# The experts' gates as three bf16 one-hot products per token, with the one-hots of four tokens side by side

## The chip, the cores and the metric

One core of a Trainium2 chip runs the whole program. The metric is the device time of one execution in microseconds (us). The core has five engines that run side by side and meet at semaphores: TensorE (PE for its matmuls, PEld for its weight loads), VectorE (DVE), ScalarE (ACT), GpSimd (POOL) and SyncE (SP, which here only issues transfers).

## What is computed

A transformer block with a hybrid mixer, memory attention and an MLP, and then a second block with a state-space mixer and a product-key expert layer (PEER), for 256 tokens of width 1024. The change touches only the expert layer. Each token picks, in each of 8 heads, 16 experts out of 128 x 128; an expert's number is a pair (i1, i2) of key numbers, and each pick has a softmax weight:

```python
i1 = jnp.take_along_axis(i_half[:, :, 0], pos // PEER_TOPK, axis=-1)
i2 = jnp.take_along_axis(i_half[:, :, 1], pos % PEER_TOPK, axis=-1)
experts = (i1 * PEER_KEYS + i2).reshape(T, PEER_HEADS * PEER_TOPK)
gates = jax.nn.softmax(best, axis=-1).reshape(T, PEER_HEADS * PEER_TOPK)
...
u = expert_u[eb].astype(xb.dtype)
act = jax.nn.gelu(jnp.einsum('td,tkd->tk', xb, u), approximate=False) * gb
return jnp.einsum('tk,tkd->td', act, expert_v[eb].astype(xb.dtype))
```

The kernel gathers nothing. It computes the hidden value of all 16,384 experts for all tokens and multiplies each by a gate, which is 0 for an expert that the token didn't pick. So it needs, for each token, a 128 x 128 matrix of gates: the sum over the token's 128 picks of weight x onehot(i1) x onehot(i2).

## The kernel before

**The weight stream.** All large weights pass through four slots in blocks of 128 x 1024 float32. SP loads a block into `raw`; ACT casts it to its high part `wh` (L516); DVE subtracts to get the low part `wl` (L1106, the "split"); PE multiplies. One block of expert up-weights is used by `up`: 24 matmuls with 256 columns moving, three for each of 8 slices (high x high, high x low, low x high), into one of two banks of `AO`. ACT takes the result through Gelu into `hid` (L948), and then casts the block that is four ahead. All matmuls go through one helper line, L2090.

**The stage of the gates.** 128 blocks of up-weights make the expert layer. The first 64 have a stage of their own. The first 29 (`PLAIN`) run while DVE does the top-k. Then come 32 rounds: in round c PE does `up` of block 29 + c and then the gates of 8 tokens (`BATCH`), one matmul per token: the one-hot rows of i2 and the weighted one-hot rows of i1, with the picks on the partitions, both float32. ACT copies the 1024 columns of the result out of the double buffer `Y` into `gstage` (L970) and sends them to DRAM (`gate_spill`), from where windows of gates come back later. DVE writes the one-hots of round c + 1 and then splits block 29 + 4 + c. The one-hots have two buffers (`hots`): round c + 1's are written once round c - 1's product is done (`g_prod`), and PE waits for them with `hot` and `hot2`. After the 32 rounds three more `up` follow, and then 128 rounds in which up and down products alternate.

**How the one-hots are written before.** `picks` holds, for every pick (partition) and token, i1, i2 and the weight in float32; ACT copies it out of PSUM after a transpose (L960). `numbers` holds 0 to 127 on each partition. For 8 tokens DVE does one TENSOR_TENSOR over 1024 elements (is i2 equal to the number, L1809) and eight TENSOR_SCALAR over 128 elements (is i1 equal, times the weight, L1814).

The order of the work is written out by hand on every engine; nothing is planned by a program.

Of the kernel before, what the change touches and what calls it, by code (L numbers as in the profile page):

```python
# [23 lines left out]
P = 128  # L24
# [3 lines left out]
BF16 = mybir.dt.bfloat16  # L28
ACT = mybir.ActivationFunctionType
ALU = mybir.AluOpType  # L30
# [4 lines left out]
T = 256  # L35
TT = T // P
# [19 lines left out]
PEER_H, TOPK, KEYS = 8, 16, 128  # L56
# [2 lines left out]
AHEAD = 64  # L59
PLAIN = 29  # L60
BATCH = 8
BATCHES = T // BATCH
WIN = 16
WINDOWS = KEYS // WIN
# [79 lines left out]
def build(nc, stream, gain_cols, cols, rows, post_gains, x, mem, meta, keys_in, out, h2_spill):  # L144
    ctx = ExitStack()
    with ctx:
        def sb(name, shape, dt=F32):
            return ctx.enter_context(nc.sbuf_tensor(name, shape, dt))
# [18 lines left out]
        masks_at = (nc.sbuf_base + 31) // 32 * 32  # L167
# [5 lines left out]
        gain = sb("gain", [P, GAINS * KT])  # L173
        stat = sb("stat", [P, 48])
        choice_at = (nc.sbuf_base + 31) // 32 * 32
        picks = sb("picks", [P, 3, T])
        numbers = sb("numbers", [P, KEYS])
        arena_at = (nc.sbuf_base + 31) // 32 * 32
        arena = sb("arena", [P, 32 * BLK])
        row_pick = sb("row_pick", [P, 32])  # L180
# [2 lines left out]
        def at(name, shape, offset, dt=F32, base=None):  # L183
            return nc.alloc_sbuf_tensor_at(name, shape, dt, offset=(arena_at if base is None else base) + offset)
# [62 lines left out]
        QP = at("QP", [P, 16, T], 8768)  # L247
        hid = at("hid", [P, AHEAD, T], 0)
        gates = at("gates", [P, 2, BATCHES, WIN * BATCH], 65536)
        hots = at("hots", [P, 2, 2, BATCH, KEYS], 98304)  # L250
        gstage = at("gstage", [P, 2, KEYS, BATCH], 114688)
        up_l = at("up_l", [P, 2, T], 98304)
        up_s = at("up_s", [P, 2, T], 100352)
# [14 lines left out]
        gsum = at("gsum", [P, 2, TT * PEER_H], 114688)  # L268
        ranks = at("ranks", [P, TOPK + 1, HK], 114816, BF16)

        peer_ah = at("peer_ah", [P, 2, T], 0, F32R, base=x_at)
        peer_al = at("peer_al", [P, 2, T], 2048, F32R, base=x_at)

# [6 lines left out]
        Y = ps("Y", [P, TT, D])  # L280
        AO = ps("AO", [P, 2, 512])
        M = ps("M", [P, 2, 512])
# [59 lines left out]
        top_sub, top_exp, top_nat, top_turn, top_T = (sem(n) for n in (  # L342
            "top_sub", "top_exp", "top_nat", "top_turn", "top_T"))
        indexed, hot, g_prod, g_out = sem("indexed"), sem("hot"), sem("g_prod"), sem("g_out")
        hot2, curve, up_part = sem("hot2"), sem("curve"), sem("up_part")
# [31 lines left out]
        TAIL = P0 + AHEAD + 2 * PAIRED  # L377
        gate_spill = nc.dram_tensor("gate_spill", (P, BATCHES, KEYS * BATCH), F32).ap()

# [125 lines left out]
        def _(act):  # L505
            step = Steps(act, act_step)
# [105 lines left out]
            for j in range(8):  # L612
                k = AG_ORDER[j]
# [342 lines left out]
            for c in range(EXP_AT, PLAIN):  # L956
                if c == FIRST_TURN:
                    act.wait_ge(top_turn, 1)
                    for j in range(TT):
                        nc.scalar.copy(picks[:, :, P * j:P * j + P],  # L960
                                       M[:, j, 0:3 * P].rearrange("p (n t) -> p n t", n=3)).then_inc(top_T, 1)
                hidden(c, P0 + c, c)
                split(P0 + 4, c)

            def gates_out(c, s):

                act.wait_ge(g_prod, c + 1)
                if not (type(c) is int and c < 2):
                    act.wait_ge(g_stored[s], (c - s) * 8)
                nc.scalar.copy(gstage[:, s, :, :],  # L970
                               Y[:, s, :].rearrange("p (t k) -> p k t", t=BATCH)).then_inc(g_out, 1)
                act.wait_ge(g_out, c + 1)
                act.dma_start(gate_spill[:, c, :], gstage[:, s, :, :].rearrange("p k t -> p (k t)"))\
                    .then_inc(g_stored[s], 16)

            def gates_in(w, first=0, n=BATCHES):

# [21 lines left out]

            for c in range(BATCHES):  # L1000
                with_gates(c, c)
                for p in range(len(PARTS)):
                    if c == PARTS[p][1] + 1:
                        part_in(p)
            for c in range(PLAIN + BATCHES, AHEAD):
                hidden(c, P0 + c, c)
# [51 lines left out]
            for w in range((KEYS - PAIRED) // WIN):  # L1058
# [10 lines left out]
                if ends[1]:  # L1069
                    for s in range(4):  # L1070
                        c = 4 * (g1 - 1) + s
# [26 lines left out]
        def _(dve):  # L1098
            step = Steps(dve, vec_step)
# [124 lines left out]
            for j in range(8):  # L1224
                split(STREAM["ag"] + 4, j)
                if j % 2:
                    c = j // 2
# [389 lines left out]
            for k in range(16):  # L1617
                c, s = divmod(k, 8)
# [114 lines left out]
            for j in range(TT):  # L1733
                for a0, a1, w, o in ROWS:
                    n = a1 - a0
# [34 lines left out]
            for j in range(TT):  # L1770
# [11 lines left out]
                for n in (8, 4, 2, 1):  # L1782
                    step.wait()
                    for half in range(2):
                        a, b = eqs[:, half, 0:n, :], eqs[:, half, n:2 * n, :]
# [18 lines left out]
            def one_hots(c):  # L1804

                s = c % 2
                if c >= 2:
                    dve.wait_ge(g_prod, c - 1)
                nc.vector.tensor_tensor(hots[:, s, 0, :, :], numbers[:, None, :].to_broadcast([P, BATCH, KEYS]),  # L1809
                                        picks[:, 1, c * BATCH:c * BATCH + BATCH][:, :, None]  # L1810
                                        .to_broadcast([P, BATCH, KEYS]), ALU.is_equal).then_inc(hot2, 1)
                for t in range(BATCH):
                    k = c * BATCH + t
                    ins = nc.vector.tensor_scalar(hots[:, s, 1, t, :], numbers[:, :], picks[:, 0, k:k + 1],  # L1814
                                                  picks[:, 2, k:k + 1], ALU.is_equal, ALU.mult)
                ins.then_inc(hot, 1)

            one_hots(0)
            for c in range(FIRST_TURN, PLAIN):
# [5 lines left out]
            for c in range(PLAIN + BATCHES, AHEAD - 1):  # L1825
                split(P0 + 4, c)
                if c < PLAIN + BATCHES + 2:
                    b = c - PLAIN - 2
# [71 lines left out]
            for w in range((KEYS - PAIRED) // WIN):  # L1900
# [10 lines left out]
                if ends[1]:  # L1911
                    for s in range(4):
                        c = 4 * (g1 - 1) + s
# [18 lines left out]
        def _(pool):  # L1932
            step = Steps(pool, pool_step)
# [131 lines left out]
            for p in range(3):  # L2065
# [10 lines left out]
            norm(5)  # L2076
            pool.wait_ge(spilled, 16)
            pool.wait_ge(tile_scaled, 3 * len(NORMS))
            nc.gpsimd.iota(numbers[:, :], [[1, KEYS]], base=0, channel_multiplier=0,
                           allow_small_or_imprecise_dtypes=True).then_inc(indexed, 1)  # L2080
            nc.gpsimd.iota(ranks[:, :, :], [[1, TOPK + 1], [0, HK]], base=0, channel_multiplier=0,
                           allow_small_or_imprecise_dtypes=True).then_inc(indexed, 1)
# [5 lines left out]
        def _(pe):  # L2088
            def mm(o, a, b, start, stop):
                return nc.tensor.matmul(o, a, b, start=start, stop=stop)  # L2090
# [352 lines left out]
            for c in range(2):  # L2443
                ins = mm(M[:, 1, P * (c + 1):P * (c + 2)], RA[:, c, :], upper[:, :], True, True)
# [102 lines left out]
            for k in range(16):  # L2547
                c, s = divmod(k, 8)
# [7 lines left out]
                for t in range(3):  # L2556
                    h = 3 * s + t
                    ins = mm(yd[:, SSD_D * h:SSD_D * h + SSD_D], MM[:, k % 2, t, :],
                             XDT[:, c, SSD_D * h:SSD_D * h + SSD_D], True, True)
# [27 lines left out]
            for j in range(14):  # L2587
                kt = (j - SC_T) % 16
                b = STREAM["wout2"] + j
                pe.wait_ge(split_lo, b + 1)  # L2590
                for c in range(TT):
                    if j < SC_T:
                        pe.wait_ge(sc_lo, j + 1)
                    else:
                        pe.wait_ge(y_lo, 3 * c + kt // 4 + 1)
                    ins = flat(b % SLOTS, [Y4[c]], [m2h[:, kt, P * c:P * c + P]], [m2l[:, kt, P * c:P * c + P]],
                               (0, 512), j == 0, False)
# [44 lines left out]
            for j in range(TT):  # L2642
                for n in range(3):
                    ins = nc.tensor.transpose(M[:, j, P * n:P * n + P], NAT[:, j, n, :], ident[:, :])
# [5 lines left out]
            def with_gates(c, s, i=0):  # L2650

                pe.wait_ge(a_free, i * 4 + (A_BASE["peer"] + PLAIN + s - 1))
                up(s, P0 + PLAIN + s, (PLAIN + s) % 2, 0, i)
                if not (type(c) is int and c < 2):
                    pe.wait_ge(g_out, c - 1)
                pe.wait_ge(hot2, c + 1)
                pe.wait_ge(hot, c + 1)
                for t in range(BATCH):
                    ins = mm(Y[:, s % 2, KEYS * t:KEYS * t + KEYS], hots[:, s % 2, 0, t, :], hots[:, s % 2, 1, t, :],
                             True, True)  # L2660
                ins.then_inc(g_prod, 1)

            for s in range(4):
# [33 lines left out]
            for j, halves in ((0, (0, 1)), (1, (0,)), (1, (1,))):  # L2697
                for s in range(2):
                    b = N_BLOCKS - 2 + s
                    pe.wait_ge(split_lo, b + 1)  # L2700
                    pe.wait_ge(hid_lo, KEYS - 1 + s + FF_CHUNKS)
                    ins = flat(b % SLOTS, [[Y4[j][h] for h in halves]], [peer_ah[:, s, P * j:P * j + P]],
                               [peer_al[:, s, P * j:P * j + P]], [512 * h for h in halves], False, s == 1)
# [75 lines left out]
```

## Time and profile before

| what | value |
|---|---|
| median of 3 runs | 1435.97 us (1435.6 to 1437.34) |
| the profiled execution's own time | 1436.53 us |
| its span in the trace | 1434.8 us |
| mean granted TensorE clock | 0.997 of full speed |
| busy in the span: PE, DVE, ACT | 1407.3, 1075.0, 794.5 us |
| the 32 rounds with gates | about 747 to 893 us from the span's start |

The profile comes from one execution; its times are counted from the start of its span. "Busy" is the time in which at least one instruction of the engine ran. Consecutive instructions of an engine overlap a little in the records, so what one costs in a row of many is read from the distance of starts, not from its own duration. A float32 matmul shows as two records, each with a weight load of its own.

### The profile page before, as it was taken

The numbers are of one execution on the slowest core, as the hardware profiler recorded it, in microseconds if no ns is written. First come the engines' busy times: TensorE is split into PE (matmuls) and PEld (weight loads), VectorE is DVE, ScalarE is ACT, GpSimd is POOL, SyncE is SP. The second block draws the span as 40 slices with busy tenths as digits, with TensorE's granted clock in tenths as the row PEclk, the third lists the DMA queues.
The fourth block names the chain that finished last, engine by engine and source line by source line (L and its number), as shares of the span: only waits on it lengthen the run. The fifth ranks groups of instructions, "written<-read, shape, count | busy, mean of one in ns | idle before, by whom it ended". The sixth has DMA issues, their size and how long they took to land.

```text
span 1434.8 us, 25922 instructions
## 1 busy us (share of the span) xinstructions
PE 1407.3 (98%) x8623; PEld 1251.4 (87%) x8623; DVE 1075.0 (75%) x2058; ACT 794.5 (55%) x1303; POOL 68.7 (5%) x66
## 2 busy tenths in 40 slices
PE   8999999999999999999999999999999999999998
PEld 8988878888898888799999999888888888888886
DVE  6996776666687588599999997666666666677776
ACT  6766764545576535455554555555555555554454
POOL 0100000000003521000000000000000000000000
PEclk9999999999999999999999999999999999999999
DMA  7533335565444523654656787657557575577754
GB/s 294 189 119 127 113 132 190 190 192 188 132 148 150 174 89 118 191 176 155 203 188 221 259 261 250 213 191 248 192 188 251 188 252 187 196 246 253 256 190 146
DMA packets 103098, 274.38 MB, mean 191 GB/s; under 512 B 8320, under 2 KB 40816, under 8 KB 102528
## 3 DMA queue, kind: packets, MB, share of 16 engines
q1 hardware_dynamic: 65024, 237.16, 49.6%
q10 hardware_dynamic: 37664, 34.37, 7.3%
q0 software_dynamic: 352, 2.11, 0.5%
q8 instruction: 32, 0.52, 0.2%
q14 instruction: 26, 0.21, 0.0%
HBM read 254.67 MB, written 18.87 MB: 191 GB/s over the span
## 4 chain that ended last, share of the span: by engine, by line
PE 85%; DVE 8%; ACT 3%; issue 1%; SPq 1%; DMA 1%; POOL 0%; DVEq 0%; ACTq 0%
PE Y L2090 43%; PE AO L2090 39%; DVE wl L1106 2%; PE M L2090 2%; DVE CV L1213 1%; ACT wh L516 1%; SPq L488 1%; DVE XS L1493 1%; DVE X L1346 0%; DVE xn L1343 0%; DVE xhl L1138 0%; DMA X<-in_x 0%; ACT xhl L559 0%; DMA raw<-in_stream 0%; ACT junk L550 0%
## 5 line engine op out<-in xcount | busy, mean ns | idle before, releaser
L1106 DVE TENSOR_TENSOR wl<-raw,wh 128x1024 fp32r<-128x1024 f32 x440 | 543.3, 1239 | 197.8 <-ACT wh L516 197.3
L2090 PE MATMUL AO<-xhl,wh 128*128 128x256 f32 (+3 forms) x2784 | 648.8, 315 | 4.6 <-DVE xhl L1138 2.6
L516 ACT CAST wh<-raw 128x1024 fp32r<-128x1024 f32 x440 | 460.8, 1050 | 146.7 <-PE Y L2090 72.5
L2090 PEld LDWEIGHTS AO<-xhl,wh 128*128 128x128 f32 x2784 | 455.3, 188 | 37.0 <-issue 3.2
L2090 PE MATMUL AO<-xhl,wl 128*128 128x256 f32 (+2 forms) x1776 | 485.0, 282 | 0.0
L2090 PEld LDWEIGHTS AO<-xhl,wl 128*128 128x128 f32 x1776 | 333.9, 188 | 7.9
L2090 PE MATMUL Y<-wh,peer_al 128*128 128x512 f32 x512 | 199.2, 389 | 0.0
L2090 PE MATMUL Y<-wl,peer_ah 128*128 128x512 f32 x512 | 199.2, 389 | 0.0
L2090 PE MATMUL Y<-wh,peer_ah 128*128 128x512 f32 x512 | 199.2, 389 | 0.0
L990 ACT CAST peer_ah<-hid 128x256 fp32r (+1 forms) x128 | 52.0, 406 | 178.3 <-DVE hid L1837 93.5
L2090 PEld LDWEIGHTS Y<-wl,peer_ah 128*128 128x128 f32 x512 | 96.1, 188 | 20.1
L2090 PEld LDWEIGHTS Y<-wh,peer_al 128*128 128x128 f32 x512 | 96.1, 188 | 20.0
L2090 PEld LDWEIGHTS Y<-wh,peer_ah 128*128 128x128 f32 x512 | 96.2, 188 | 17.6
L1843 DVE TENSOR_TENSOR peer_al<-hid,peer_ah 128x256 fp32r<-128x256 f32 x128 | 54.4, 425 | 71.7 <-ACT peer_ah L990 71.5
L948 ACT ACTIVATE hid<-AO 128x256 f32<-128x256 f32 (+1 forms) x64 | 24.6, 384 | 90.9 <-PE AO L2090 90.8
L1814 DVE TENSOR_SCALAR hots<-numbers,picks 128x128 f32<-128x128 f32 x256 | 68.3, 340 | 0.0
L2090 PE MATMUL Y<-hots 128*128 128x128 f32 x512 | 62.3, 275 | 0.0
L2090 PEld LDWEIGHTS Y<-hots 128*128 128x128 f32 x512 | 60.0, 192 | 0.0
L1962 POOL TENSOR_SCALAR stat<-stat 128x1 f32<-128x1 f32 x12 | 6.6, 548 | 1087.5 <-ACT fin_j L1084 814.6
L1837 DVE TENSOR_TENSOR hid<-hid,gates (+1 forms) x128 | 53.4, 417 | 1.6 <-issue 0.7
L2090 PE MATMUL Y<-wh,mlp_ah 128*128 128x512 f32 x128 | 50.1, 391 | 1.2 <-DVE mlp_al L1415 1.2
L1213 DVE SCALAR_TENSOR_TENSOR CV<-UP,colp,CV 128x256 f32<-128x256 f32 x120 | 49.8, 475 | 0.3 <-ACT CV L604 0.3
(354 smaller groups left out, 1610.4 us busy)
## 6 DMA issues: line engine op xcount, KB each, us to landing
raw<-in_stream SPq DMA_DIRECT2D x440, 512.0 KB, 3.3
gate_spill<-gstage ACTq DMA_DIRECT2D x32, 512.0 KB, 4.9
gates<-gate_spill ACTq DMA_DIRECT2D x6, 2048.0 KB, 15.2
gates<-gate_spill ACTq DMA_DIRECT2D x6, 512.0 KB, 7.1
rowg<-in_post SPq DMA_DIRECT2D x3, 512.0 KB, 4.3
X<-in_x SPq DMA_DIRECT2D x2, 512.0 KB, 5.0
memx<-in_mem SPq DMA_DIRECT2D x1, 1024.0 KB, 7.6
keys<-in_keys POOLq DMA_DIRECT2D x1, 1024.0 KB, 7.0
```

What stands on the lines that cost most here:

```text
L488: sp.dma_start(RV[o:o + 1, :, :].bitcast(F32), RS[f:f + HG, c, :].bitcast(F32)).then_inc(lines_in, 16)
L516: nc.scalar.copy(wh[:, s, :], raw[:, s, :]).then_inc(split_hi, 1)
L948: nc.scalar.activation(hid[:, c, :], AO[:, s % 2, 0:T], ACT.Gelu).then_inc(a_free, 1)
L990: nc.scalar.copy(peer_ah[:, s, :], hid[:, slot, :]).then_inc(hid_hi, 1)
L1106: nc.vector.tensor_tensor(wl[:, s, :], raw[:, s, :], wh[:, s, :].bitcast(F32), ALU.subtract)\
L1213: nc.vector.scalar_tensor_tensor(out=CV[:, c, :], in0=src, scalar=col("conv_w", c * CONV_W + w), in1=CV[:, c, :], op0=ALU.mult, op1=ALU.ad ...
L1493: nc.vector.scalar_tensor_tensor(out=dst, in0=src, scalar=wt, in1=dst, op0=ALU.mult, op1=ALU.add).then_inc(xconv, 1)
L1814: ins = nc.vector.tensor_scalar(hots[:, s, 1, t, :], numbers[:, :], picks[:, 0, k:k + 1], picks[:, 2, k:k + 1], ALU.is_equal, ALU.mult)
L1837: nc.vector.tensor_tensor(h, h, gates[:, w % 2, :, bass.ds(k * BATCH, BATCH)], ALU.mult)\
L1843: nc.vector.tensor_tensor(peer_al[:, s, :], hid[:, slot, :], peer_ah[:, s, :].bitcast(F32), ALU.subtract).then_inc(hid_lo, 1)
L1962: nc.gpsimd.tensor_scalar(stat[:, dst:dst + 1], stat[:, src:src + 1], EPS, None, ALU.add).then_inc(done, 1)
L2090: return nc.tensor.matmul(o, a, b, start=start, stop=stop)
```

## The change

The gate matrix of a token becomes three bf16 matmuls that add up in PSUM. The stationary side of each is the plain one-hot of i2, the same for all three; the moving side is the one-hot of i1 times one of three bf16 parts of the weight (the weight rounded to bf16, the rest rounded again, and what is left), which together make the weight. DVE writes the plain one-hots of i1 and i2 for 8 tokens with one TENSOR_TENSOR of 2048 bf16 elements into `found`, waits for it, and writes the three weighted ones with three TENSOR_TENSOR of 1024 bf16 elements into `spread`. The elements of four tokens (`QUAD`) lie side by side, so that a token's row of 128 is read by PE with a step of four elements (8 bytes). ACT writes `picks` in bf16, and DVE makes the weight's second and third part once, in the first round. `numbers` becomes 128 x 4 bf16 elements, each number four times. All buffers that change lie in memory that was free at that time; the arena starts at the same address.

```diff
-        picks = sb("picks", [P, 3, T])
-        numbers = sb("numbers", [P, KEYS])
+        picks = sb("picks", [P, BATCHES, 2 * 5, QUAD], BF16)
+        rest = sb("rest", [P, TT, P])
...
-        hots = at("hots", [P, 2, 2, BATCH, KEYS], 98304)
+        spread = at("spread", [P, 2, 3, 2, KEYS, QUAD], 98304, BF16)
+        found = at("found", [P, 2, 4, KEYS, QUAD], 122880, BF16)
...
+        numbers = at("numbers", [P, KEYS, QUAD], 0, BF16, base=masks_at)
...
-                        nc.scalar.copy(picks[:, :, P * j:P * j + P],
-                                       M[:, j, 0:3 * P].rearrange("p (n t) -> p n t", n=3)).then_inc(top_T, 1)
+                        b = BATCHES // TT * j
+                        nc.scalar.copy(picks[:, b:b + BATCHES // TT, 0:6, :].rearrange("p b (n h) q -> p b n (h q)", n=3),
+                                       M[:, j, 0:3 * P].rearrange("p (n b t) -> p b n t", n=3, t=BATCH)).then_inc(top_T, 1)
...
-                nc.vector.tensor_tensor(hots[:, s, 0, :, :], numbers[:, None, :].to_broadcast([P, BATCH, KEYS]),
-                                        picks[:, 1, c * BATCH:c * BATCH + BATCH][:, :, None]
-                                        .to_broadcast([P, BATCH, KEYS]), ALU.is_equal).then_inc(hot2, 1)
-                for t in range(BATCH):
-                    k = c * BATCH + t
-                    ins = nc.vector.tensor_scalar(hots[:, s, 1, t, :], numbers[:, :], picks[:, 0, k:k + 1],
-                                                  picks[:, 2, k:k + 1], ALU.is_equal, ALU.mult)
+                nc.vector.tensor_tensor(found[:, s, :, :, :], numbers[:, None, :, :].to_broadcast([P, 4, KEYS, QUAD]),
+                                        picks[:, c, 0:4, None, :].to_broadcast([P, 4, KEYS, QUAD]), ALU.is_equal)\
+                    .then_inc(hot2, 1)
+                if c == 0:
+                    parts_of_weights()
+                dve.wait_ge(hot2, c + 1)
+                for n in range(3):
+                    ins = nc.vector.tensor_tensor(spread[:, s, n, :, :, :], found[:, s, 0:2, :, :],
+                                                  picks[:, c, 4 + 2 * n:6 + 2 * n, None, :]
+                                                  .to_broadcast([P, 2, KEYS, QUAD]), ALU.mult)
                 ins.then_inc(hot, 1)
+
+            def parts_of_weights():
+
+                w = [picks[:, :, 4 + 2 * n:6 + 2 * n, :].rearrange("p b h q -> p b (h q)") for n in range(3)]
+                r = rest[:, :, :].rearrange("p j (b t) -> p (j b) t", t=BATCH)
+                for j in range(TT):
+                    b = slice(BATCHES // TT * j, BATCHES // TT * (j + 1))
+                    step(nc.vector.tensor_tensor(r[:, b, :], M[:, j, 2 * P:3 * P].rearrange("p (b t) -> p b t", t=BATCH),
+                                                 w[0][:, b, :], ALU.subtract))
+                step.wait()
+                step(nc.vector.tensor_copy(w[1], r))
+                step.wait()
+                step(nc.vector.tensor_tensor(w[2], r, w[1], ALU.subtract))
+                step.wait()
...
-            nc.gpsimd.iota(numbers[:, :], [[1, KEYS]], base=0, channel_multiplier=0,
+            nc.gpsimd.iota(numbers[:, :, :], [[1, KEYS], [0, QUAD]], base=0, channel_multiplier=0,
...
                 for t in range(BATCH):
-                    ins = mm(Y[:, s % 2, KEYS * t:KEYS * t + KEYS], hots[:, s % 2, 0, t, :], hots[:, s % 2, 1, t, :],
-                             True, True)
+                    h, q = divmod(t, QUAD)
+                    for n in range(3):
+                        ins = mm(Y[:, s % 2, KEYS * t:KEYS * t + KEYS], found[:, s % 2, 2 + h, :, q],
+                                 spread[:, s % 2, n, h, :, q], n == 0, n == 2)
                 ins.then_inc(g_prod, 1)
```

On DVE, at the start of the rounds, stood before (the last row of the top-k, the last split ahead of it, and rounds 0 and 1):

```order
L1794 TENSOR_TENSOR NAT<-BV,gsum 128x128
L1106 TENSOR_TENSOR wl<-raw,wh 128x1024 [waits split_hi]
L1809 TENSOR_TENSOR hots<-numbers,picks 128x1024 [waits top_T]
L1814 TENSOR_SCALAR hots<-numbers,picks 128x128 x8
L1106 TENSOR_TENSOR wl<-raw,wh 128x1024 [waits split_hi]
```

and stands now, with the round that then repeats as the last four rows:

```order
L1813 TENSOR_TENSOR found<-numbers,picks 128x2048 [waits top_T]
L1831 TENSOR_TENSOR rest<-M,picks 128x128 x2
L1834 CAST picks<-rest 128x32x8 [waits vec_step]
L1836 TENSOR_TENSOR picks<-rest,picks 128x32x8 [waits vec_step]
L1820 TENSOR_TENSOR spread<-found,picks 128x1024 [waits hot2,vec_step]
L1820 TENSOR_TENSOR spread<-found,picks 128x1024 x2
L1106 TENSOR_TENSOR wl<-raw,wh 128x1024 [waits split_hi]
L1813 TENSOR_TENSOR found<-numbers,picks 128x2048 [waits g_prod]
L1820 TENSOR_TENSOR spread<-found,picks 128x1024 [waits hot2]
L1820 TENSOR_TENSOR spread<-found,picks 128x1024 x2
```

Nine instructions of a round become four, the second of which waits for the first, and four instructions with three waits stand once in the first round, ahead of the first product.

On PE, at the end of one round's `up` and the start of the next, stood before:

```order
L2090 MATMUL AO<-xhl,wh 128x256 x2
L2090 MATMUL AO<-xhl,wl 128x256
L2090 MATMUL Y<-hots 128x128 [waits hot,hot2]
L2090 MATMUL Y<-hots 128x128 x7
L2090 MATMUL AO<-xhl,wh 128x256 [waits split_lo,a_free]
```

and stands now:

```order
L2111 MATMUL AO<-xhl,wh 128x256 x2
L2111 MATMUL AO<-xhl,wl 128x256
L2111 MATMUL Y<-spread,found 128x128 [waits hot,hot2]
L2111 MATMUL Y<-spread,found 128x128 x23
L2111 MATMUL AO<-xhl,wh 128x256 [waits split_lo,a_free]
```

Eight float32 matmuls of a round become 24 bf16 matmuls at the same place, with the same waits.

## Rows read from the trace of the kernel before

**Rows 1.** The page: busy time, share of the span and instructions of each engine
```profile
PE 1407.3 (98%) x8623; PEld 1251.4 (87%) x8623; DVE 1075.0 (75%) x2058; ACT 794.5 (55%) x1303; POOL 68.7 (5%) x66
```

**Rows 2.** The chain that ended last, 735 to 920 us: start, us, what
```profile
741.82 5.68 PE AO L2090 x48
747.50 1.78 PE Y L2090 x16
749.29 2.84 PE AO L2090 x24
...
890.93 1.78 PE Y L2090 x16
```

**Rows 3.** Busy time of each engine in the stretch of the rounds
```profile
747.50:892.72 145.22, 145.22 (x1259) 145.22 (x1258) 136.48 (x311) 73.78 (x95) 0.00 (x0) 1.00 0.76 248
```

**Rows 4.** Instructions on the tile hots: ns min/median/max, first and last start us
```profile
L2090 PEld LDWEIGHTS Y<-hots x512: 189/192/192, 747.2 to 892.3; 128*128 128x128 f32 x171
L2090 PE MATMUL Y<-hots x512: 272/275/275, 747.3 to 892.4; 128*128 128x128 f32 x171
```

**Rows 5.** Timeline of DVE, an early and a late round: start, us, what
```profile
747.20 1.22 DVE L1809 TENSOR_TENSOR hots<-numbers,picks 128x1024 f32<-128x1024 f32 x1
748.33 2.14 DVE L1814 TENSOR_SCALAR hots<-numbers,picks 128x128 f32<-128x128 f32 x8
750.38 1.22 DVE L1106 TENSOR_TENSOR wl<-raw,wh 128x1024 fp32r<-128x1024 f32 x1
751.52 1.22 DVE L1809 TENSOR_TENSOR hots<-numbers,picks 128x1024 f32<-128x1024 f32 x1
...
883.06 1.23 DVE L1106 TENSOR_TENSOR wl<-raw,wh 128x1024 fp32r<-128x1024 f32 x1 [0.21 <-ACT wh L516]
```

**Rows 6.** Timeline of DVE in the top-k, instructions on bf16 tiles
```profile
709.11 2.36 DVE L1773 TENSOR_TENSOR eqs<-PF,ranks 128x2048 bf16<-128x2048 bf16 x2
...
712.97 1.22 DVE L1779 TENSOR_TENSOR eqs<-eqs,I16B 128x2048 bf16<-128x2048 bf16 x1
...
717.51 1.28 DVE L1787 TENSOR_TENSOR eqs<-eqs 128x1024 bf16<-128x1024 bf16 x2
...
724.57 0.29 DVE L1787 TENSOR_TENSOR eqs<-eqs 128x256 bf16<-128x256 bf16 x1
724.89 0.49 DVE L1787 TENSOR_TENSOR NAT<-eqs 128x128 f32<-128x128 bf16 x2
```

**Rows 7.** TensorE where less than 128 columns move per load, and its cheapest full load
```profile
507.20 0.78 PE L2090 MATMUL Y<-XDT,MM 128*128 128x64 f32 x6
507.81 0.86 PE L2090 MATMUL M<-ST,XS 128*128 128x384 f32 x2
421.56 0.54 PEld L2090 LDWEIGHTS M<-dtz,upper 128*128 128x128 f32 x4
L2180 PEld LDWEIGHTS M<-ident x128: 138/140/231, 2.6 to 375.7; 128*128 128x128 f32 x128
```

**Rows 8.** Around the first round, and DVE instructions like the new ones there
```profile
740.27 0.63 DVE L1794 TENSOR_TENSOR NAT<-BV,gsum 128x128 f32<-128x128 f32 x2
741.86 0.86 ACT L960 COPY picks<-M 128x384 f32<-128x384 f32 x2 [0.22 <-PE M L2644]
742.82 1.22 DVE L1809 TENSOR_TENSOR hots<-numbers,picks 128x1024 f32<-128x1024 f32 x1
...
898.09 0.29 DVE L1830 COPY gates<-gstage 128x256 f32<-128x256 f32 x1
...
901.25 0.43 DVE L1837 TENSOR_TENSOR hid<-hid,gates 128x256 f32<-128x256 f32 x1
```

**Rows 9.** The busiest window of transfers in the rounds, and the spill's landing
```profile
789.00:805.00 16.00, 16.00 (x141) 16.00 (x140) 15.12 (x37) 8.48 (x12) 0.00 (x0) 1.00 0.93 302
gate_spill<-gstage ACTq DMA_DIRECT2D x31, 512.0 KB, 4.9
```

More of the change, by code:

```diff
@@ L61 @@
 BATCH = 8
+QUAD = BATCH // 2
 BATCHES = T // BATCH
```

## The prediction

> **What bounds the kernel now.** The page's busy times come first: PE is busy for 1407 of 1434.8 us, DVE for 1075 [rows 1]. That is an average over many stages, so next the chain that ended last, at the place of the change. From 741.82 to 892.7 us it holds nothing but PE: 2.84 us of `up` (24 matmuls on AO), 1.78 us of gate products (16 records on Y), and so on, 32 times [rows 2]. The window of just this stretch agrees: PE busy for 145.22 of 145.22 us, DVE for 136.48, ACT for 73.78 [rows 3]. So a round takes 2.84 + 1.78 = 4.62 us, PE's work alone sets it, and whatever shortens the product shortens the round, until another engine's round is longer.
>
> The next engine is DVE, and the timeline says how close it is. Early in the stage it is never idle: it starts one-hots at 747.20 and the next at 751.52, so its own round takes 4.32 us (1.13 for L1809, 2.05 for the eight L1814, 1.14 for the split). Later it idles some 0.2 us per round for ACT's cast, because PE only frees a slot every 4.62 us [rows 5]. DVE is thus 0.30 us per round off being the bound. The reader should see that a faster product alone could give only those 0.30 us; what DVE's new round costs decides as much.
>
> **PE's part.** Removed: 8 float32 matmuls per round, 16 records in 1.78 us, 111.5 ns each [rows 2, 4]. Added: 24 bf16 matmuls that each load 128 columns and move 128. No row shows a bf16 matmul, so it is bounded.
> - What moves: a float32 matmul of 128 columns costs 223 ns here (two records), one of the fp32r matmuls of `up` moves 256 columns in 2.84 / 24 = 118.3 ns [rows 2]. Half of that is 59 ns for 128 columns; a quarter of 223 is 56.
> - What loads: where little moves, the load sets the pace. Six records with 64 float32 columns start at 507.20 and the next form at 507.81, 102 ns each, though 64 columns move in half of what 128 need, 56 ns. Four loads with only 24 columns moving take 0.54 us, and one takes 0.19, so 0.35 / 3 = 117 ns apart [rows 4, 7]. A float32 load therefore costs 102 to 117 ns, and if a bf16 load did too, the new product would be slower. But the load of the transposes, also 128 columns, is 140 ns long where the others are 189 to 192, some 50 ns less [rows 4, 7]: a full load can be had for about 52 to 67 ns, which hides nearly behind 59.
>
> I take 59 ns, because bf16 is half the bytes of float32 and so nearer to the short load; the bounds are 56 and 117. The product costs 24 x 59 = 1.42 us, PE's round 2.84 + 1.42 = 4.26 us, 0.36 less. It breaks even at 1.78 / 24 = 74 ns.
>
> On this the Trainium skill speaks with two voices. Its page "TensorE: Matmul & The Clock Gate", section "Back-to-back issue gap", gives some 81 ns per matmul of 128 columns in a stream in which every matmul has a load, and 56 ns without loads; by 81 the product would be 1.94 us and the kernel about 5 us slower. The same page, section "LDWEIGHTS (loading the stationary operand)", has a load take its columns / 1.2 ns, 107 ns here, which the float32 rows fit and the transposes' row doesn't; by that the kernel would be some 25 us slower. Its section "Weight-path perf modes — Fast Weight Load (FWL) and DoubleRow" promises a cheaper load for types other than FP32. No row here can choose between them.
>
> **DVE's part.** All lengths come from the top-k, which has bf16 instructions of just these sizes, one of them with one operand spread over a dimension [rows 6]. Two of 2048 elements take 2.36 us and one takes 1.22, so they start 1.14 apart and overlap by 0.08. Two of 1024 take 1.28, so they start 0.60 apart. An instruction that waits for the one before it starts 0.03 after its end (724.57 + 0.29 to 724.89). The new round: `found` 1.22 + 0.03, three `spread` 3 x 0.60, the split 1.14 as before, in all 4.19 us against 4.32. Not shown is an operand whose rows of 4 elements are read over and over. If that cost nothing, 4.19 stands; if all four lost the doubled bf16 rate, the round would be the float32 one, 2.27 + 3 x 1.14 + 1.14 = 6.83 us. I take 4.19, since L1779, with rows of 8 and an operand read over and over, keeps the rate.
>
> So PE's 4.26 stays just above DVE's 4.19. If DVE gets 0.1 longer than this, it is the bound.
>
> **The first round.** ACT's two copies have as many elements as before and let DVE start at 742.82 [rows 8]. Then `found` 1.25, two subtractions of 128 elements 0.63 + 0.03, a cast of 256 0.29 + 0.03, a subtraction of 256 0.43 + 0.03, three `spread` 0.60 + 0.60 + 0.68: ready at 747.39, where PE's product began at 747.50 by the chain, with its first load at 747.2 [rows 2, 4, 8]. PE may stand for 0 to 0.4 us, I take 0.2. Behind it DVE's split and second one-hots end at about 747.4 + 1.1 + 1.25 + 1.9 = 751.6, and PE's second product is due at 747.6 + 4.26 = 751.9, so the wait isn't repeated.
>
> **What costs nothing.** ACT does what it did: 73.78 us in 145 [rows 3]; shorter rounds leave it over 1.9 us free in each. The larger iota of `numbers` on GpSimd runs long before the top-k ends. Transfers: a round moves as many bytes in 4.26 us as in 4.62, so the mean share of 0.76 becomes 0.82 [rows 3]; a window of 16 us with 0.93 and 302 GB/s left PE fully busy [rows 9]. A spill lands in 4.9 us [rows 9], and its buffer is used again two rounds later, 8.5 us less the copy. With that cover gone, ACT's copy would wait, and its cast, DVE's split and PE's `up` behind it.
>
> **The sum.** 32 x (1.78 - 1.42) = 11.5 us less, or 11.8 unrounded (1.784, 1.416), and 0.2 more for the first round: -11.6. The profiled execution took 1436.53 us, so 1424.9, and it lies 0.56 above the median: 1424.4 us, by the median of the runs shown.
>
> **The rivals.**
> - **The load sets the pace of the products (slower).** A bf16 load costs what a float32 one does, 102 to 117 ns. The product takes 2.45 to 2.81 us, each round 0.67 to 1.03 more than before: +21 to +33 us, 1457 to 1469. For it: both float32 rows where little moves [rows 7]. Against it: the transposes' shorter load. Chance 0.10.
> - **The load, or the 8-byte step in which PE reads, is hidden in part.** 68 to 85 ns, around the middle between 59 and 102: the product takes 1.63 to 2.04 us, -5 to +8 us, 1431 to 1444. No row has PE read with a step. Chance 0.11: 0.04 of it faster, 0.02 no change, 0.05 slower.
> - **DVE becomes the bound.** The wait for `found` or the short rows cost 0.1 to 0.3 us more: rounds of 4.3 to 4.5 us, 1426 to 1432. Rows 5 speak for it: DVE has so little to spare. Chance 0.08. If the bf16 rate is lost, rounds of 6.83 us, +70 us, 1506: chance 0.04.
> - **The gain is hidden behind the transfers.** The rounds stay near 4.5 to 4.6 us since the spill and the weight stream come no faster: 1432 to 1436. The landing time of 4.9 us speaks against it. Chance 0.04, half of it no change.
>
> **How the numbers follow.** My forecast has the remaining 0.63; its own range is 1422 to 1429 (56 ns, where DVE's 4.19 is the floor and 0.43 x 31 = 13.3 us is the most to be had; 66 ns). Down to 1421 if DVE is a little cheaper, and up to 1437 with the longer DVE round, the transfers and the better half of the partly hidden load, it is 0.63 + 0.08 + 0.04 + 0.06, about 8 in 10. Changes of under 0.2% (2.9 us) are about what a measurement of this kernel can't tell from none. Faster by more: 0.63 + 0.08 + 0.02 + 0.04 = 0.77; within: 0.02 + 0.02 = 0.04; slower: 0.10 + 0.05 + 0.04 = 0.19.
>
> **What would show it.** In the profile after: 24 records on Y per round, 59 ns apart, and rounds 4.26 us long in the chain. If the chain's pieces on Y are longer than 1.78 us, the load rival holds, and PEld starts will be over 74 ns apart. If `found` is longer than 1.3 us or `spread` than 0.75, or the chain leaves PE for DVE's `spread`, it is DVE. If ACT waits before L970 for `g_stored`, it is the transfers. At the start, PE's idle time before the first product should be under 0.4 us. The most likely mistake is the price of a bf16 matmul with its load, which rests on no row of its own kind.

## The result, and the profile after

The changed kernel is slower: 1470.28 us, the median of 4 runs (1469.26 to 1471.28), against 1435.78 us of the kernel before (4 runs, 1434.68 to 1437.34). The ratio is 1.0239, with a 95% interval of 1.0222 to 1.0257. The prediction, 1424.4 us and so a gain, had the wrong sign, and the result lies 33 us above its range.

The page of the changed kernel, its busy times (those of before are in [rows 1]):

```profile
span 1467.4 us, 26279 instructions
PE 1441.0 (98%) x8879; PEld 1283.4 (87%) x8879; DVE 1074.4 (73%) x1902; ACT 794.7 (54%) x1303; POOL 69.6 (5%) x66
```

DVE and ACT are as busy as before to within 1 us; PE has 34 us more. The chain that ended last at the first rounds, beside [rows 2] (start us, us, what):

```profile
746.35 2.85 PE Y L2111 x24
749.20 2.84 PE AO L2111 x24
752.03 2.85 PE Y L2111 x24
```

It is PE alone, as before. `up` (AO) has kept its 2.84 us; a product (Y) takes 2.85 us where it took 1.78 and where 1.42 were forecast. Its 24 matmuls are 2.85 / 24 = 119 ns apart, twice the 59 ns of the prediction. (Times per matmul below are such pieces of the chain divided by the number of matmuls.) The window of the stretch, beside [rows 3] (stretch, us, busy us and instructions of PE, PEld, DVE, ACT and POOL, granted clock, DMA share, GB/s):

```profile
746.35:927.00 180.65, 180.65 (x1528) 177.85 (x1527) 136.27 (x157) 74.94 (x96) 0.00 (x0) 1.00 0.58 202
```

PE never idles, and the clock is at its full level of 2.4 GHz. The 32 rounds, from 746.35 to where `up` follows the last product at 925.36, take 179.0 us instead of 145.2: 33.8 more, and 32 x (2.85 - 1.78) gives 34. The span grew by 32.6, since this execution came to its first product 1.15 us earlier. So the whole loss is in the product, and nothing came back or was lost elsewhere.

Who uses the new tiles (duration ns min/median/max, first and last start us):

```profile
L2111 PEld LDWEIGHTS Y<-spread,found x768: 111/117/137, 746.2 to 924.9; 128*128 128x128 bf16 x192
L2111 PE MATMUL Y<-spread,found x768: 282/298/302, 746.2 to 925.1; 128*128 128x128 bf16 x192
L1820 DVE TENSOR_TENSOR spread<-found,picks x96: 683/686/695, 744.1 to 916.5; 128x1024 bf16<-128x1024 bf16 x96
L1813 DVE TENSOR_TENSOR found<-numbers,picks x32: 1218/1226/1228, 741.6 to 914.0; 128x2048 bf16<-128x2048 bf16 x32
```

A load record is now 117 ns long, and the matmuls of a product are 119 ns apart. From these rows alone the load looks guilty: this is just what the load rival forecast (102 to 117 ns apart, 1457 to 1469 us). But PEld starts once per matmul whichever of the two is late, so neither its spacing nor the 98% of the stretch in which it is "busy" says who waits for whom. PE reads both sides with the step of 8 bytes, and only experiments separate three causes: the load itself, the step of the loaded side, the step of the moving side.

### The profile page after: what moved, and what is told of

It is laid out like the page before. It is cut to its first block, busy times and chain, and to the rows that moved or that the text cites. A ratio compares the mean times of both kernels' runs of the same rounds, so it can differ in the third digit from the quotient of the medians.

```text
span 1467.4 us, 26279 instructions
## 1 busy us (share of the span) xinstructions
PE 1441.0 (98%) x8879; PEld 1283.4 (87%) x8879; DVE 1074.4 (73%) x1902; ACT 794.7 (54%) x1303; POOL 69.6 (5%) x66
## 4 chain that ended last, share of the span: by engine, by line
PE 86%; DVE 8%; ACT 3%; issue 1%; SPq 1%; DMA 1%; POOL 0%; DVEq 0%; ACTq 0%
PE Y L2111 44%; PE AO L2111 38%; DVE wl L1110 2%; PE M L2111 2%; DVE CV L1217 1%; ACT wh L519 1%; SPq L491 1%; DVE XS L1497 1%; DVE X L1350 0%; DVE xn L1347 0%; DMA X<-in_x 0%; DVE xhl L1142 0%; ACT xhl L562 0%; DMA raw<-in_stream 0%; ACT junk L553 0%
## 5 line engine op out<-in xcount | busy, mean ns | idle before, releaser
L2111 PE MATMUL Y<-spread,found 128*128 128x128 bf16 x768 | 96.1, 297 | 0.0
L2111 PEld LDWEIGHTS Y<-spread,found 128*128 128x128 bf16 x768 | 85.5, 117 | 2.8
L1820 DVE TENSOR_TENSOR spread<-found,picks 128x1024 bf16<-128x1024 bf16 x96 | 60.7, 688 | 1.1
L974 ACT COPY gstage<-Y 128x1024 f32<-128x1024 f32 x32 | 32.5, 1015 | 47.9 <-PE Y L2111 47.9
```

Of the source, the lines that this page charges most:

```text
L974: nc.scalar.copy(gstage[:, s, :, :], Y[:, s, :].rearrange("p (t k) -> p k t", t=BATCH)).then_inc(g_out, 1)
L1820: ins = nc.vector.tensor_tensor(spread[:, s, n, :, :, :], found[:, s, 0:2, :, :], picks[:, c, 4 + 2 * n:6 + 2 * n, None, :] .to_broadcast( ...
```

## The experiments

Three theories stood at the start: (A) the step of 8 bytes on the moving side (`spread`) slows the matmul; (B) the step on the stationary side (`found`) slows the load; (C) a bf16 load costs as much as a float32 one in any layout. Where no number of runs is given, there was one. Each group of runs has its own time of the kernel before beside it; across groups, small differences are read from the traces' rows and not from the times.

**One side at a time, then both.** A token's 128 elements are read from 128 neighbouring places of the same buffers, the step being kept on the other side.

```diff
 # moving side close together (and, for the stationary side, the same with found)
-                                 spread[:, s % 2, n, h, :, q], n == 0, n == 2)
+                                 spread[:, s % 2, n, h, :, :].rearrange("p k q -> p (k q)")[:, KEYS * q:KEYS * q + KEYS], n == 0, n == 2)
```

Expected with the moving side close together:

> PE takes the moving side of each bf16 product from 128 elements that lie close together in the same buffer; the stationary side keeps its step of four elements, and DVE writes as before. The output is not the reference's, since the elements read are not a token's. Theory A (reading the moving side with an 8-byte step halves its rate): the matmuls start 56 to 65 ns apart, a round is 4.2 to 4.4 us, the time near 1425 to 1430 us. Theory B (the stepped stationary load sets the pace) and theory C (any bf16 load of 128 columns costs about 118 ns): the pieces on Y stay 2.85 us, 1468 to 1472 us.

Expected with the stationary side close together:

> The stationary side alone is read from 128 elements close together; the moving side keeps the step of four. The output is not the reference's. Theory A (moving step): no change, 118 ns per matmul, 1468 to 1472 us. Theory B (stepped load): 56 to 65 ns per matmul, 1425 to 1430 us. Theory C (any bf16 load): no change.

Expected with both:

> Both sides are read from elements close together. The output is not the reference's. Theories A and B: 56 to 65 ns per matmul, 1425 to 1430 us, even where only one of the sides mattered or both must be close. Theory C (any bf16 load of 128 columns costs 118 ns): no change, 1468 to 1472 us.

Measured: 1424.43, 1468.5 and 1422.85 us, beside 1434.93 for the kernel before. The chain of the kernel with the moving side close together:

```profile
802.26 1.38 PE Y L2111 x24
803.63 2.89 PE AO L2111 x24
```

and its load records, whose stationary side is still stepped:

```profile
L2111 PEld LDWEIGHTS Y<-spread,found x768: 110/113/133, 746.6 to 880.2; 128*128 128x128 bf16 x192
```

The chain with only the stationary side close together, and its load records:

```profile
800.99 2.83 PE AO L2111 x24
803.83 2.79 PE Y L2111 x24
```
```profile
L2111 PEld LDWEIGHTS Y<-spread,found x768: 95/115/118, 747.5 to 924.2; 128*128 128x128 bf16 x192
```

and with both sides close together, its chain and its load records:

```profile
802.40 2.89 PE AO L2111 x24
805.29 1.36 PE Y L2111 x24
```
```profile
L2111 PEld LDWEIGHTS Y<-spread,found x768: 95/98/100, 745.7 to 878.6; 128*128 128x128 bf16 x192
```

One edit of the moving side brings the product from 2.85 to 1.38 us and the kernel from 1470 to 1424 us; the other edit takes 0.06 us off the product. The matmuls are where theory A put them, and B and C fall; the times, 1424.43 and 1422.85 us, are 1 to 2 us under the 1425 to 1430 expected. Load records of 113 ns stand beside matmuls that are 57 ns apart, so a record's length isn't what a load costs in a row of many, just as [rows 4] had 189 ns records 111.5 ns apart. Nor does the length tell of the load's own step: side by side the records are 98 ns long where the moving side is close together too, and 115 ns where it isn't. The step of the stationary side lengthens a record from 98 to 113 ns and costs 0.02 us of the product (1.38 against 1.36 us). What a bf16 load costs by itself no run shows: in such a row it is hidden at 57 ns.

The prediction had weighed two figures of the page "TensorE: Matmul & The Clock Gate" of the Trainium skill. Its section "Back-to-back issue gap" gives 81 ns for a matmul of 128 columns in a stream with loads and some 56 ns without them, and its section "LDWEIGHTS (loading the stationary operand)" gives 107 ns for the load. The trace agrees with neither 81 nor 107: here each of the 24 matmuls had a load of 128 columns, and they were 57 ns apart.

**Which step is dear?** Both sides at 4 bytes; the moving side at 6 bytes (96 places, so some tokens share columns); the moving side at 16 bytes (over both groups of four). Number and shape of the instructions stay.

```diff
 # moving side at 6 bytes; at 16 bytes the same with u=8 over both groups of four
+                                 spread[:, s % 2, n, h, 0:96, :].rearrange("p k q -> p (k q)").rearrange("p (k u) -> p k u", u=3)[:, :, min(q, 2)], n == 0, n == 2)
```

Expected at 4, 6 and 16 bytes:

> Both sides are read with a step of two elements (4 bytes) in place of four (8 bytes). The output is not the reference's. If the cost of a step grows with the bytes that it passes over, the matmuls are between 60 and 100 ns apart, 1426 to 1458 us; if any step breaks the pairs of bf16 elements, 118 ns as with four, 1468 to 1472 us; theory C: no change.

> The change with the moving side read with a step of three elements (6 bytes), the stationary side still four. The output is not the reference's. If the rate falls once a step passes over more than 4 bytes, 118 ns per matmul and 1468 to 1470 us; if it falls in proportion from 4 bytes on, about 88 ns and 1447 us; if it falls only at 8 bytes, 58 ns and 1424 us.

> The change with the moving side read with a step of eight elements (16 bytes), the stationary side still four. The output is not the reference's. If the half rate at four elements is a second level that holds for every longer step, 118 ns and 1468 to 1470 us; if the cost grows in proportion to the bytes, some 225 ns, products of 5.4 us per round and about 1555 us.

Measured: 1423.9, 1449.02 and 1615.7 us. One product in the chain of each, in this order:

```profile
805.62 1.39 PE Y L2111 x24
```
```profile
807.57 2.16 PE Y L2111 x24
809.73 2.86 PE AO L2111 x24
```
```profile
757.88 5.54 PE Y L2111 x24
763.42 4.22 PE AO L2111 x24
...
803.27 4.71 PE AO L2111 x24
807.98 5.54 PE Y L2111 x24
```

| step of the moving side, bytes | 2 | 4 | 6 | 8 | 16 |
|---|---|---|---|---|---|
| ns per matmul of 128 bf16 columns | 57 | 58 | 90 | 119 | 231 |
| the same / (128 columns x step), ns per column and byte | 0.22 | 0.113 | 0.117 | 0.116 | 0.113 |

(The column of 2 bytes is the run with the moving side close together, that of 8 bytes the change itself.) Up to 4 bytes the step is free; the run with 4 bytes missed its expectation, which had no price under 60 ns. From there the time of a column is 0.113 to 0.117 ns times the step in bytes, as if PE ran over the memory from the first to the last element, 16 bytes in 1.8 to 1.9 ns. A price per line of 16 bytes that is touched would give the same table; only a step of more than 16 bytes would tell the two apart, and no run has one. The page "SBUF — State Buffer" of the Trainium skill, section "Door 1: The DMA port swizzle (why `[64,N]` ≈ `[32,N]`)", has lines of 16 bytes that run at full rate from two hits per line on, with 8 bf16 elements as the free distance. For what TensorE moves, the table says otherwise: at 8 bytes two elements lie in a line, and the rate is half; it is full with four.

The kernel with 16 bytes missed its expectation of 1555 us by 60, for a reason of its own; it stands in the last section.

**Bytes or elements?** In the kernel before, `up` in the rounds reads its 256 moving columns, which are rounded float32 (fp32r) of 4 bytes, with a step of two elements, so 8 bytes.

```diff
-                up(s, P0 + PLAIN + s, (PLAIN + s) % 2, 0, i)
+                pe.wait_ge(split_lo, i * 4 + (P0 + PLAIN + s + 1))
+                wide_into(AO[:, (PLAIN + s) % 2, 0:T], (P0 + PLAIN + s) % SLOTS, stepped(0), stepped(1), T).then_inc(w_used, 1)
```

> The kernel before, with its float32 products, but the fp32r moving side of `up` in the 32 rounds is read with a step of two elements (8 bytes, the step of the change in bytes). Those hidden values are not the reference's. If it is the bytes of the step that halve the rate, `up` takes about 24 x 225 = 5.4 us in place of 2.84 and the time is about 1517 us; if it is the number of elements (four), nothing changes: 1435 us.

Measured: 1521.1 us (before: 1435.48). The chain:

```profile
801.03 1.79 PE Y L2090 x16
802.82 5.48 PE AO L2090 x24
```

5.48 / 24 = 228 ns for 256 columns instead of 118.3: 0.89 ns per column at 8 bytes, where bf16 has 0.93. So it is the bytes of the step that count and not the number of elements, and another type pays nearly the same.

**And the float32 product of before?** Its moving side with a step of two elements, 8 bytes as well:

```diff
-                    ins = mm(Y[:, s % 2, KEYS * t:KEYS * t + KEYS], hots[:, s % 2, 0, t, :], hots[:, s % 2, 1, t, :],
+                    ins = mm(Y[:, s % 2, KEYS * t:KEYS * t + KEYS], hots[:, s % 2, 0, t, :],
+                             hots[:, s % 2, 1, :, :].rearrange("p (g v) k -> p g (v k)", v=2)[:, t // 2, :]
+                             .rearrange("p (k u) -> p u k", u=2)[:, t % 2, :],
```

> The kernel before with its float32 products, whose moving side alone is read with a step of two elements (8 bytes). The gates are not the reference's. If the price is the bytes passed over in every pass over the operand, each record takes twice as long, 3.57 us per round on Y, and the time is about 1492 us; if the four times slower float32 product hides the slower reading, 1435 us.

```profile
802.11 1.82 PE Y L2090 x16
```

1436.04 us beside 1437.11 of the kernel before (whose runs spread from 1434.34 to 1437.48), and 1.82 us for the product instead of 1.78. So the step is hidden, but only just. A record takes 1.82 / 16 = 113.8 ns instead of 111.5, and the `up` with the 8-byte step paid 228 ns for 256 columns, 114 for 128. The rows fit this reading: each of a float32 matmul's two records fetches its 128 columns at the price of the step, which is hardly more than what the record takes anyway. A longer step of a float32 operand wasn't run. For bf16, whose matmul takes 57 ns, the same 8 bytes are a doubling.

**The whole computation with a free step.** The one-hots of two tokens side by side instead of four, which makes the step 4 bytes. DVE has as many instructions with as many elements, but its re-read rows are 2 long.

```diff
-QUAD = BATCH // 2
+QUAD = 2
+SETS = BATCH // QUAD
...
-        picks = sb("picks", [P, BATCHES, 2 * 5, QUAD], BF16)
+        picks = sb("picks", [P, BATCHES, 5 * SETS, QUAD], BF16)
...
-        spread = at("spread", [P, 2, 3, 2, KEYS, QUAD], 98304, BF16)
-        found = at("found", [P, 2, 4, KEYS, QUAD], 122880, BF16)
+        spread = at("spread", [P, 2, 3, SETS, KEYS, QUAD], 98304, BF16)
+        found = at("found", [P, 2, 2 * SETS, KEYS, QUAD], 122880, BF16)
```

> The change with two tokens side by side in place of four (QUAD = 2), complete and with the reference's output: PE reads both sides with a step of two elements (4 bytes), DVE writes rows of two. Theory A (the 8-byte step of the moving side is the whole loss): products 58 ns apart, 1.39 us on Y per round, and 1424 us if DVE keeps 1.22 us for found and 0.69 for spread. Rival: with rows of two elements DVE loses its doubled rate on the operand that is read over and over, its round grows from 4.2 to 4.6 us or more (up to 6.8), and the time is 1436 us or more (up to 1507).

Measured: 1425.37 us (4 runs, 1424.1 to 1426.67) against 1435.48 (7 runs): ratio 0.9925, interval 0.9909 to 0.9942. The chain:

```profile
800.10 1.39 PE Y L2112 x24
801.49 2.89 PE AO L2112 x24
```

its window of 100 us in the rounds (columns as above), and DVE's two groups of instructions on the new tiles (duration ns min/median/max):

```profile
770.00:870.00 100.00, 100.00 (x1132) 98.98 (x1131) 99.18 (x120) 55.04 (x71) 0.00 (x0) 1.00 0.81 277
```
```profile
L1821 DVE TENSOR_TENSOR spread<-found,picks x96: 681/685/695, 746.5 to 877.9; 128x1024 bf16<-128x1024 bf16 x96
L1814 DVE TENSOR_TENSOR found<-numbers,picks x32: 1215/1217/1220, 744.0 to 875.4; 128x2048 bf16<-128x2048 bf16 x32
```

The complete computation now gains 10 us, 0.75%, on the kernel before, nearly the 11.6 us that the prediction had for the layout with 8 bytes. A DVE instruction takes the same whether its re-read rows are 2 or 4 elements long (685 ns against 686, 1217 against 1226). DVE is busy for 99% of the window, so its round is hardly shorter than PE's 4.28 us.

**Where is DVE's limit?** Again pairs. First PE multiplies only the first of the three parts while DVE writes all three, so that PE is out of the way:

```diff
-                    for n in range(3):
+                    for n in range(1):
                         ins = mm(Y[:, s % 2, KEYS * t:KEYS * t + KEYS], found[:, s % 2, SETS + h, :, q],
-                                 spread[:, s % 2, n, h, :, q], n == 0, n == 2)
+                                 spread[:, s % 2, n, h, :, q], n == 0, n == 0)
```

> Two tokens side by side; DVE writes all three weighted one-hots as before, but PE uses only the first, so the gates are those of the weight rounded to bf16. It asks what DVE's round is once PE no longer covers it. If DVE's round is 4.20 us as added up in the prediction, the rounds become 4.20 us, DVE is never idle and the time is 1422 to 1424 us. If DVE isn't the next bound, PE's round of 2.89 + 0.46 = 3.35 us gives about 1396 us.

Measured: 1423.89 us (before: 1437.11). The chain is DVE's all through the rounds:

```profile
803.83 1.15 DVE found L1814
804.98 0.02 issue
805.00 1.90 DVE spread L1821 x3
806.90 1.14 DVE wl L1111
808.03 1.14 DVE found L1814
```

A round is 808.03 - 803.83 = 4.20 us, where the prediction had 4.19 for DVE. Without two thirds of PE's products the kernel is 13 us faster than the one before, where the complete kernel with pairs is 10 us faster: DVE's 4.20 us leave no more than 0.08 us per round below PE's 4.28.

**Less work on both.** The third part of the weight is left out on DVE and on PE, with pairs and with fours:

```diff
-                for n in range(3):
+                for n in range(2):
                     ins = nc.vector.tensor_tensor(spread[:, s, n, :, :, :], ...
...
-                    for n in range(3):
+                    for n in range(2):
                         ins = mm(Y[:, s % 2, KEYS * t:KEYS * t + KEYS], ...
```

> Two tokens side by side (as in the run with pairs), and the third bf16 part of the weight is left out: two products per token, two spread writes per round. If PE's round is 2.89 + 16 x 0.058 = 3.82 us and DVE's is 4.20 - 0.60 = 3.60 us, PE stays the bound and the time is 1425.4 - 32 x (4.275 - 3.82) = 1411 us. If DVE or the transfers set the round already at 4.2 us, 1423 us.

> The change as it is (four tokens side by side, PE reads with an 8-byte step), with the third part of the weight left out on DVE and PE: 16 products per round. If each stepped matmul costs 118.5 ns whatever their number, the product takes 1.90 us, the round 4.74 us and the time is about 1439 us, still no gain against the kernel before; if a fixed cost per round were behind the loss, it would be about 1450 us.

Measured: 1410.45 us with pairs (4 runs, 1409.39 to 1412.66; ratio 0.9821, interval 0.9803 to 0.9839) and 1438.22 us with fours, one run, beside 1437.11. The chains:

```profile
801.33 0.94 PE Y L2112 x16
```
```profile
802.40 1.90 PE Y L2111 x16
```

16 matmuls are 59 ns apart with a step of 4 bytes and 119 with one of 8, the same prices as with 24 of them. With the step of 8 bytes, even two thirds of the changed kernel's products only draw level with the float32 ones. The window of the pairs (columns as above) shows DVE with room again:

```profile
770.00:870.00 100.00, 100.00 (x1048) 98.93 (x1047) 91.66 (x101) 58.20 (x78) 0.00 (x0) 1.00 0.89 307
```

PE is still fully busy with 307 GB/s beside it, a transfer share of 0.89.

## Why the prediction was wrong

**The failed step: what moves, in "PE's part".** It priced 128 bf16 columns as half of the 118.3 ns of `up`, 59 ns. That row has its 256 columns side by side, 4 bytes apart; those of `spread` are 8 bytes apart. With the moving side at 2 or 4 bytes the price is 57 to 58 ns, so the sum was right for a layout that the change doesn't have; with 8 bytes it is 119. The product takes 2.85 us and not 1.42, 1.43 us more per round and 46 us in 32: the forecast of 1424.4 us and these 46 give 1470.

**The rival that named the step was given too low a price.** It said that no row has PE read with a step, and then gave 68 to 85 ns as around the middle between 59 and 102, which is 80.5. Nothing in the trace supported that end: the 102 was a price of float32 loads and says nothing of a step. For an access that no row shows, half the rate should have been among the bounds, with a chance. The argument from the elements (128 columns are 128 columns) took the place of one from the bytes between them.

**The load rival had the time, and not the mechanism.** 102 to 117 ns and 1457 to 1469 us nearly hit the result. The load records are 113 to 117 ns long, and the loads still pass at 57 ns with the moving side close together. The prediction's own marks for this rival, pieces on Y over 1.78 us and PEld starts over 74 ns apart, both came true and would have misled: there is one load per matmul, and its starts have the matmuls' pace whichever of the two is slow.

**What held.** DVE: 4.19 us forecast for its round, 4.20 measured, where it is the limit; row lengths of 4 cost nothing. In the changed kernel it has the round of 4.20 us only at first (`found` starts at 747.04 and 751.24); late in the stage it idles 1.03 us per round for ACT's cast and 0.27 us for PE's product, since the rounds have PE's length:

```profile
884.12 1.22 DVE L1110 TENSOR_TENSOR wl<-raw,wh 128x1024 fp32r<-128x1024 f32 x1 [1.03 <-ACT wh L519]
885.61 1.23 DVE L1813 TENSOR_TENSOR found<-numbers,picks 128x2048 bf16<-128x2048 bf16 x1 [0.27 <-PE Y L2111]
```

The first round: PE's stall of 0 to 0.4 us was 0, as DVE was ready with `spread` before PE was:

```profile
741.65 1.22 DVE L1813 TENSOR_TENSOR found<-numbers,picks 128x2048 bf16<-128x2048 bf16 x1
...
744.09 1.89 DVE L1820 TENSOR_TENSOR spread<-found,picks 128x1024 bf16<-128x1024 bf16 x3
```

This took 744.09 + 1.89 - 741.65 = 4.33 us instead of 4.57 and ended at 745.98, PE's product began at 746.35. Transfers: fully hidden, in the kernel with rounds of 3.82 us too. PE's round, forecast at 4.26 us, is 4.28 in the kernel with pairs, its product 1.39 us by the chain instead of 1.42 and its `up` 2.89 instead of 2.84. That `up` seems 0.05 us longer than in the changed kernel comes from where the chain divides PE's time, at the ends of matmuls, which are modelled. The starts of the matmuls, in the changed kernel and then with pairs, show no difference:

```profile
751.88 3.01 PE L2111 MATMUL Y<-spread,found 128*128 128x128 bf16 x24
754.63 0.49 PE L2111 MATMUL AO<-xhl,wh 128*128 128x256 f32 x2
757.56 3.00 PE L2111 MATMUL Y<-spread,found 128*128 128x128 bf16 x24
```
```profile
799.94 1.55 PE L2112 MATMUL Y<-spread,found 128*128 128x128 bf16 x24
801.30 0.48 PE L2112 MATMUL AO<-xhl,wh 128*128 128x256 f32 x2
804.22 1.55 PE L2112 MATMUL Y<-spread,found 128*128 128x128 bf16 x24
```

From `up`'s first start to the next product's it is 2.93 and 2.92 us, from the product's to `up`'s 2.75 and 1.36.

## What to carry to other kernels

Before several tokens, heads or channels are laid side by side so that VectorE can write long rows, work out the step in bytes that this leaves to TensorE's moving operand: here up to 4 bytes were free, and beyond that a matmul took 0.11 to 0.12 ns per column and byte of the step, while the loaded operand bore 8 bytes at almost no cost. A matmul that is slow by its type can hide the step, as the float32 one hid 8 bytes here; the cost then appears only with the faster type, and looks like the faster type's own. A busy load engine proves nothing as long as its starts have the matmuls' pace: put one operand close together at a time and see which one moves the spacing.

## What the hardware showed that was not expected

**A price per byte of distance.** 57, 58, 90, 119 and 231 ns for 128 columns at steps of 2, 4, 6, 8 and 16 bytes, and 0.89 to 0.93 ns per column at 8 bytes for two types.

**The clock fell while PE was 100% busy.** In the kernel with 16 bytes, the windows (columns as above) of the last two `up` ahead of the rounds, the first product, the second product and the `up` behind it, an `up` and a product 40 us on, and 4 us soon after the last product, which ends at 1069.53:

```profile
742.83:748.50 5.67, 5.67 (x50) 5.62 (x49) 5.57 (x10) 2.19 (x4) 0.00 (x0) 1.00 0.51 173
748.51:754.05 5.54, 5.54 (x25) 3.03 (x24) 4.95 (x6) 1.32 (x2) 0.00 (x0) 0.88 0.29 98
757.88:763.42 5.54, 5.54 (x26) 2.98 (x24) 1.23 (x1) 1.32 (x2) 0.00 (x0) 0.96 0.30 93
763.42:767.60 4.18, 4.18 (x25) 4.14 (x25) 3.12 (x4) 1.02 (x1) 0.00 (x0) 0.65 0.32 129
803.27:807.98 4.71, 4.71 (x25) 4.65 (x25) 3.12 (x4) 1.02 (x1) 0.00 (x0) 0.57 0.28 114
808.00:813.50 5.50, 5.50 (x25) 3.07 (x24) 1.23 (x1) 1.32 (x2) 0.00 (x0) 0.75 0.29 95
1076.00:1080.00 4.00, 4.00 (x36) 3.95 (x35) 2.55 (x5) 1.38 (x3) 0.00 (x0) 1.00 0.43 139
```

PE is busy in every one of them, yet the granted clock falls from 2.4 GHz (1.00) to a mixture with 1.2 GHz (0.57 to 0.75 40 us on). It begins to fall in the first product (0.88), and it is back at 1.00 within 10 us of the last one. What PE did as it fell was to move 24 times 128 columns in 5.54 us, a quarter of the pace that it has with a free step. The product takes 5.54 us at 0.96 and at 0.75 alike. The `up` behind it pays, 4.22 and then 4.71 us instead of 2.84: the 31 `up` between the products take 144 us in the chain where 31 x 2.84 would be 88, and these 56 us are most of the 60 by which 1615.7 us exceeded the expected 1555. With 8 bytes the clock stayed at 1.00. This rests on one run, and no other was made to vary it.

**A float32 matmul hid the step of 8 bytes**, with 1.82 us for eight tokens instead of 1.78.
